# Reordering the attention stage of a hybrid residual block: the two heads of a pair one after the other on ScalarE, half a gate item between their suffix sums

## The reference

```
xn = rmsnorm(x); proj = xn @ w_in          # q,k,v of A | q,k,v, i, f, o of B | q of C | 3 x 1024 gate columns
A  stick-breaking attention, 8 heads x 64, causal (s < t):
   z = q k / 8;  log_keep = log_sigmoid(-z);  suffix = sum of log_keep over later s
   a = exp(log_sigmoid(z) + suffix);  y_sb = a v
B  mLSTM, 4 heads x 128, then rmsnorm per head and sigmoid(o):  y_ml
C  attention on 256 memory tokens, 4 heads x 128, q and k normed, softmax:  y_mem
merged = sum over branches of sigmoid(gate_b) * (y_b @ w_b);  h = x + merged @ w_out
h = h + PEER(rmsnorm(h))                   # 16384 one-neuron experts, 8 heads, top 16
```

## Time and profile before

| | us |
|---|---|
| median of three runs | 1521.15 (1515.63 to 1523.68) |
| the profiled execution | 1526.73 |
| its span | 1525.0 |
| PE busy | 1482.0 (97%) |
| DVE busy | 1103.5 (72%) |
| ACT busy | 749.7 (49%) |
| POOL busy | 423.0 (28%) |

### The profile page before, as it was taken

The page is one execution under the profiler, slowest core; times in us unless marked ns, Lnnn a source line. Parts: engine busy times, 40 slices in busy tenths (PEclk is TensorE's granted clock), DMA queues, the critical chain, the costliest instruction groups (busy, mean ns, idle before and its releaser), DMA issues.

```text
span 1525.0 us, 22189 instructions
## 1 busy us (share of the span) xinstructions
PE 1482.0 (97%) x7430; PEld 1216.5 (80%) x7430; DVE 1103.5 (72%) x1890; ACT 749.7 (49%) x939; POOL 423.0 (28%) x188
## 2 busy tenths in 40 slices
PE   7989999999889999999999999999999999999999
PEld 5768777777768888888888888888888888888887
DVE  6884542774957999999699999544666666666665
ACT  6343476646544544444465655544444444444442
POOL 4656523433545578779300000000000000000000
PEclk9999999999989999999999999999999999999999
DMA  5434533325633366666588888897988888888984
GB/s 195 159 122 143 198 104 104 104 83 217 239 124 111 111 214 221 207 215 219 204 311 300 290 315 304 310 322 241 326 293 285 296 285 288 294 285 290 299 280 147
DMA packets 166704, 345.14 MB, mean 226 GB/s; under 512 B 13420, under 2 KB 78956, under 8 KB 164336
## 3 DMA queue, kind: packets, MB, share of 16 engines
q1 hardware_dynamic: 166640, 344.32, 66.3%
HBM read 268.76 MB, written 75.51 MB: 226 GB/s over the span
## 4 chain that ended last, share of the span: by engine, by line
PE 65%; DVE 13%; issue 1%; POOL 1%; ACT 1%; ACTq 0%
PE ps L1144 30%; PE ps L1135 24%; PE ps L1173 4%; PE ps L728 2%; PE ps L1016 1%; DVE top_lists L1967 1%; DVE top_lists L1960 1%; POOL u_r L495 1%; DVE top_in L1961 1%; DVE top_lists L1964 1%; DVE top_lists L1957 1%; DVE mergedT L1890 1%; PE ps L751 1%; DVE h_scaled L1920 1%; PE ps L690 1%
## 5 line engine op out<-in xcount | busy, mean ns | idle before, releaser
L1135 PE MATMUL ps<-hT_r,u_r 128*128 128x512 f32 x2048 | 470.7, 390 | 0.1
L1144 PE MATMUL ps<-v_r,w_pairs 128*128 128x512 f32 x2036 | 461.7, 389 | 0.0
L1135 PEld LDWEIGHTS ps<-hT_r,u_r 128*128 128x128 f32 x2048 | 382.7, 188 | 79.8 <-POOL u_r L495 0.5
L1144 PEld LDWEIGHTS ps<-v_r,w_pairs 128*128 128x128 f32 x2036 | 382.3, 188 | 79.2
L459 POOL TENSOR_TENSOR w_r<-w_raw,w_r 128x1024 fp32r<-128x1024 f32 x93 | 238.5, 2569 | 263.6 <-ACT w_r L1259 174.4
L2106 DVE TENSOR_TENSOR v_r<-vraw,v_r 128x1024 fp32r<-128x1024 f32 x128 | 156.9, 1226 | 148.3 <-ACT v_r L1549 148.3
L1549 ACT ACTIVATE v_r<-vraw 128x1024 fp32r<-128x1024 f32 x128 | 135.7, 1060 | 253.6 <-PE ps L1144 248.7
L1496 ACT ACTIVATE act_stage<-ps 128x512 f32<-128x512 f32 x128 | 76.6, 599 | 227.6 <-PE ps L1135 227.6
L495 POOL TENSOR_TENSOR u_r<-uraw,u_r 128x1024 fp32r<-128x1024 f32 x60 | 172.9, 2892 | 46.7 <-ACT u_r L1477 46.4
L728 PE MATMUL ps<-xT_r,w_r 128*128 128x512 f32 x648 | 158.8, 400 | 8.6 <-DVE pre_stage L1703 4.4
L1259 ACT ACTIVATE w_r<-w_raw 128x1024 fp32r<-128x1024 f32 x99 | 103.9, 1055 | 104.2 <-PE ps L751 46.7
(11 more groups left out here) (261 smaller groups left out, 1510.4 us busy)
## 6 DMA issues: line engine op xcount, KB each, us to landing
uraw<-in_u SPq DMA_DIRECT2D x128, 512.0 KB, 4.7
vraw<-in_v SPq DMA_DIRECT2D x128, 512.0 KB, 5.3
w_raw<-in_w SPq DMA_DIRECT2D x100, 512.0 KB, 3.5
acts_out<-act_stage SPq DMA_DIRECT2D x128, 256.0 KB, 2.3
gates<-stage SPq DMA_DIRECT2D x16, 2048.0 KB, 7.4
g_in<-gates SPq DMA_DIRECT2D x64, 512.0 KB, 6.4
act_in<-acts_out SPq DMA_DIRECT2D x128, 256.0 KB, 5.3
gates_pre<-pre_stage SPq DMA_DIRECT2D x24, 256.0 KB, 2.4
```

The costliest lines, as they stand in the source:

```text
L1135: ins = pe.matmul(bank(s % 2), u2[s][:, w, k * P:(k + 1) * P], hr4[:, w, k, :], start=i == 0, stop=i == 15, skip_group_check=True)
L1144: ins = pe.matmul(bank(2 * q + h), w2[:, s, w, q * P:(q + 1) * P], v2[s][:, w, h * BANK:(h + 1) * BANK], start=start and w == 0, stop=stop ...
```

## The change

On PE `gate_item` is split in `gate_high` and `gate_low`; in each pair the high half of gate item m+2 goes between the suffix sums of the two heads. On ACT the heads of a pair go one after the other: Abs, Exp and Ln of the first, a weight item, Abs and Exp of the second, the high copy of the first, Ln of the second, a weight item, the high copy of the second; the two Exp of the sums and the third weight item as before. On DVE `take_y(p-1)` and the low part of the first head go ahead of the second `keep`, and `take_gate(m+1)` ahead of the second `low_part`. The norms of mem_q and mem_k go to the ends of the first and second pair. Behind the pairs `take_gate(16)` goes ahead of `decay(3)` and `take_gate(20)` ahead of the reduction; the gating of y_ml goes ahead of `take_gate(23)`; the low part of y_sb goes behind the third head's take in branch C. ACT makes the high part of the third branch item ahead of the high part of y_mem, which now waits for the first low part of `y_r`.

```diff
--- before.py
+++ after.py
@@ -822,11 +822,22 @@
                     n_item(n, n % 2, j, 4 * (1 - b % 2), xr4, TT)
             pe.wait_ge(n_out, 3 * TT)
 
-            def gate_item(m):
+            def gate_high(m):
 
                 at_least(pe, pre_out, m - (m == GATE_ASIDE))
                 n = gate_at(m)
-                t_item(n, n % 2, gate_bank(m), xr4)
+                high_ready(n)
+                t_part(n % 2, gate_bank(m), xr4, 0)
+
+            def gate_low(m):
+
+                n = gate_at(m)
+                take_item(n)
+                t_part(n % 2, gate_bank(m), xr4, 1)
+
+            def gate_item(m):
+                gate_high(m)
+                gate_low(m)
 
             for j in range(4):
                 n_item(V_AT[j], V_AT[j] % 2, j, 4, mr4, MT)
@@ -904,8 +915,9 @@
                 sb_suffix(2 * p)
                 if p == PAIRS - 1:
                     turn_rows()
+                gate_high(m + 2)
                 sb_suffix(2 * p + 1)
-                gate_item(m + 2)
+                gate_low(m + 2)
             pe.wait_ge(cols_out, 1)
             sb_values(PAIRS - 1)
             gate_item(16)
@@ -939,7 +951,7 @@
                 gate_item(18 + h)
 
 
-            pe.wait_ge(qk_normed, 1)
+            pe.wait_ge(qk_normed, 2)
             pe.wait_ge(num_out, MLH)
             for h in range(NH):
                 for t in range(TT):
@@ -1319,17 +1331,17 @@
             def region(s):
                 return ps[:, s * 3 * BANK:s * 3 * BANK + CAUSAL]
 
-            def ln_pair(p):
-
-                act.wait_ge(z_ready, p + 1)
-                for h in range(2):
-                    step(act.activation(lk[h], region(h), ACT.Abs))
-                for h in range(2):
-                    act.wait_ge(act_step, steps[0] - 1)
-                    step(act.activation(lk[h], lk[h], ACT.Exp, scale=-1.0))
-                for h in range(2):
-                    act.wait_ge(act_step, steps[0] - 1 + h)
-                    act.activation(lk[h], lk[h], ACT.Ln, bias=1.0).then_inc(ln_ready, 1)
+            def abs_part(h):
+
+                step(act.activation(lk[h % 2], region(h % 2), ACT.Abs))
+
+            def exp_abs(h):
+                act.wait_ge(act_step, steps[0])
+                step(act.activation(lk[h % 2], lk[h % 2], ACT.Exp, scale=-1.0))
+
+            def ln_part(h):
+                act.wait_ge(act_step, steps[0])
+                act.activation(lk[h % 2], lk[h % 2], ACT.Ln, bias=1.0).then_inc(ln_ready, 1)
 
             def hi_part(h):
                 act.wait_ge(*((keep_ready, h + 1) if h < 2 else (keep_summed, h - 1)))
@@ -1346,11 +1358,18 @@
 
             act.activation(roots[:, 61:62], eps_col[:, :], ACT.Exp)
             for p in range(PAIRS):
-                ln_pair(p)
                 n = I_G + GATES_IN_KV + 3 * p + 2
+                act.wait_ge(z_ready, p + 1)
+                abs_part(2 * p)
+                exp_abs(2 * p)
+                ln_part(2 * p)
+                high_ws(n)
+                abs_part(2 * p + 1)
+                exp_abs(2 * p + 1)
                 hi_part(2 * p)
+                ln_part(2 * p + 1)
+                high_ws(n + 1)
                 hi_part(2 * p + 1)
-                high_ws(n, n + 1)
                 exp_part(2 * p)
                 exp_part(2 * p + 1)
                 high_ws(n + 2)
@@ -1368,7 +1387,7 @@
             act.activation(roots[:, S_ML:S_H], sums[:, S_ML:S_H], ACT.Sqrt, bias=eps_col[:, :],
                            scale=1.0 / HD).then_inc(ml_rooted, 1)
             high_ws(I_G + 22)
-            act.wait_ge(qk_normed, 1)
+            act.wait_ge(qk_normed, 2)
             for h in range(NH):
                 act.wait_ge(qkT_done, h + 1)
                 act.activation(mem_qT3[:, h, :], bank(h), ACT.Copy, scale=qg_scaled[:, 0:1]).then_inc(qkT_out, 1)
@@ -1409,8 +1428,9 @@
 
             act.wait_ge(mlT_out, MLH)
             act.activation(y_r[:, 4096:6144], y_mlT, ACT.Copy, scale=1.0 / SPREAD).then_inc(y_hi, 1)
+            high_w(I_BR + 2, (I_BR + 2) % 4)
             act.wait_ge(my_out, NH)
-            act.wait_ge(y_lo, 2)
+            act.wait_ge(y_lo, 1)
             act.activation(y_r[:, 8192:10240], y_memT, ACT.Copy, scale=1.0 / SPREAD).then_inc(y_hi, 1)
 
 
@@ -1429,9 +1449,10 @@
                                scale=1.0 / SPREAD).then_inc(m_hi, 1)
 
             for p in range(12):
-                high_w(I_BR + p + 2, (I_BR + p + 2) % 4)
                 if p == 0:
                     gate_of(0)
+                else:
+                    high_w(I_BR + p + 2, (I_BR + p + 2) % 4)
                 if p >= 9:
                     merged_hi(p - 9)
                 if p < 11:
@@ -1715,18 +1736,21 @@
             for t in range(MT):
                 dve.tensor_scalar(mem_v3[:, t, :], bank(4 + t), rstd[:, TT + t:TT + t + 1], None,
                                   ALU.mult).then_inc(n_out, 1)
-            dve.wait_ge(qk_rooted, 1)
-            link(dve.reciprocal(rstd[:, S_Q:S_ML], roots[:, S_Q:S_ML]))
+            take_gate(3)
 
             def spread(col, n, m):
 
                 return col.unsqueeze(2).broadcast_to([P, n, m])
 
-            q_ = mem_q.rearrange("p (g c) -> p g c", c=HD)
-            k_ = mem_k.rearrange("p (g c) -> p g c", c=HD)
-            dve.tensor_tensor(q_, q_, spread(rstd[:, S_Q:S_K], 16, HD), ALU.mult)
-            dve.tensor_tensor(k_, k_, spread(rstd[:, S_K:S_ML], 8, HD), ALU.mult).then_inc(qk_normed, 1)
-            take_gate(3)
+            def norm_q():
+                dve.wait_ge(qk_rooted, 1)
+                link(dve.reciprocal(rstd[:, S_Q:S_ML], roots[:, S_Q:S_ML]))
+                q_ = mem_q.rearrange("p (g c) -> p g c", c=HD)
+                dve.tensor_tensor(q_, q_, spread(rstd[:, S_Q:S_K], 16, HD), ALU.mult).then_inc(qk_normed, 1)
+
+            def norm_k():
+                k_ = mem_k.rearrange("p (g c) -> p g c", c=HD)
+                dve.tensor_tensor(k_, k_, spread(rstd[:, S_K:S_ML], 8, HD), ALU.mult).then_inc(qk_normed, 1)
 
             def region(s):
                 return ps[:, s * 3 * BANK:s * 3 * BANK + CAUSAL]
@@ -1771,22 +1795,26 @@
                 m = GATES_IN_KV + 3 * p
                 take_gate(m)
                 keep(2 * p)
-                keep(2 * p + 1)
-                low_part(2 * p)
                 if p >= 1:
                     take_y(p - 1)
+                low_part(2 * p)
+                keep(2 * p + 1)
+                take_gate(m + 1)
                 low_part(2 * p + 1)
-                take_gate(m + 1)
                 if p == PAIRS - 1:
                     dve.wait_ge(cols_turned, 1)
                     dve.tensor_copy(key_cols[:, :], bank(6)[:, 0:32]).then_inc(cols_out, 1)
                     decay(0)
                     decay(1)
                 take_gate(m + 2)
+                if p == 0:
+                    norm_q()
+                elif p == 1:
+                    norm_k()
             take_y(PAIRS - 1)
             decay(2)
+            take_gate(16)
             decay(3)
-            take_gate(16)
 
             def weigh(h):
                 dve.wait_ge(e_masked, h + 1)
@@ -1819,17 +1847,22 @@
                     take_gate(18)
             dve.wait_ge(num_out, MLH)
             link(dve.tensor_tensor(squares, y_ml, y_ml, ALU.mult))
+            take_gate(20)
             dve.tensor_reduce(sums[:, S_ML:S_H], squares.rearrange("p (g c) -> p g c", c=HD), AX.X,
                               ALU.add).then_inc(ml_squared, 1)
-            take_gate(20)
-            dve.wait_ge(ml_rooted, 1)
-            link(dve.reciprocal(rstd[:, S_ML:S_H], roots[:, S_ML:S_H]))
             y_ = y_ml.rearrange("p (g c) -> p g c", c=HD)
-            link(dve.tensor_tensor(y_, y_, spread(rstd[:, S_ML:S_H], 16, HD), ALU.mult))
-            dve.wait_ge(sig_o, 1)
-            dve.scalar_tensor_tensor(out=y_ml, in0=y_ml, scalar=SPREAD, in1=ml_o, op0=ALU.mult,
-                                     op1=ALU.mult).then_inc(ml_normed, 1)
-
+
+            def scale_ml():
+                dve.wait_ge(ml_rooted, 1)
+                link(dve.reciprocal(rstd[:, S_ML:S_H], roots[:, S_ML:S_H]))
+                link(dve.tensor_tensor(y_, y_, spread(rstd[:, S_ML:S_H], 16, HD), ALU.mult))
+
+            def gate_ml():
+                dve.wait_ge(sig_o, 1)
+                dve.scalar_tensor_tensor(out=y_ml, in0=y_ml, scalar=SPREAD, in1=ml_o, op0=ALU.mult,
+                                         op1=ALU.mult).then_inc(ml_normed, 1)
+
+            scale_ml()
             take_gate(21)
 
 
@@ -1848,11 +1881,14 @@
                 p_ = probs[h % 2].rearrange("p (t m) -> p t m", m=MEM)
                 dve.tensor_tensor(p_, p_, spread(den[:, 16 + n4:20 + n4], 4, MEM), ALU.mult).then_inc(mp_ready, 1)
 
+            def low_y(b):
+                dve.wait_ge(y_hi, b + 1)
+                dve.scalar_tensor_tensor(out=y_r[:, b * 4096 + 2048:(b + 1) * 4096],
+                                         in0=y_r[:, b * 4096:b * 4096 + 2048].bitcast(F32), scalar=1.0 - SPREAD,
```

(20 more changed lines are left out.)

## The result

| | before | after |
|---|---|---|
| median, us | 1521.61 (four runs, 1515.63 to 1523.68) | 1532.32 (four runs, 1531.67 to 1533.82) |
| the profiled execution, us | 1526.73 | 1533.82 |
| its span, us | 1525.0 | 1532.1 |
| ScalarE, GpSimd busy, us | 749.7, 423.0 | 760.5, 418.1 |

The account below looks back on a forecast made before the run. TensorE was taken as what everything waits for in the attention stage; work terms summed to +4.5 us, slow clock added 6: +10.5, rounded to +10 on the median 1521.15, so 1531 us, 8 in 10 range 1517 to 1539.

Parts of the forecast that it names:

- Entry: First pair: moving the norms lets TensorE go on 2.5 us earlier, all given back; next pair's gate item +1.7 us.
- The take behind the second keep: In each pair, VectorE's late emptying of bank 7 makes TensorE wait before the gate half; the take is 4.6 us late.
- The cycle at full clock: One pair after the change, without slow clock: 27.8 us with 6.2 us of pauses, against 23.4 us in the old order.
- Table loads: ScalarE in each pair: every change between Exp and Ln costs a load, four instead of two, 16 in the stage.
- The clock: One slow-clock stretch of 1.5 us behind each of four long TensorE pauses: +6 us, bounds 0 and +12.
- The last pair: Fourth pair, to the first mLSTM scores: 31.1 us instead of 28.62, +2.5 us before any slow clock.
- mLSTM, memory, to the third branch item: Behind the pairs, earlier takes, moved gating and low part, and an earlier weight copy: -0.6, -0.4 and -3.4 us.
- From 458 us on: The change touches nothing from 458 us to the end; a change there of more than 2 us would show it wrong.
- rival of spared pairs: Pairs: POOL does not hold the small sums, each of three pairs 1.9 us shorter, clock possibly spared; about 1523 us, chance 0.30.
- rival of table sets: ScalarE in the pairs: one set serves Exp and Ln, so all loads inside the pair go; 1517 us, chance 0.10.
- That of the slow clock: Pairs: TensorE stays at the lower clock through most of the suffix sums, +6 us more; 1537 us, chance 0.10.

Follow-up runs that it names:

- the pauses filled: The changed kernel with sixteen never-read matmuls behind the first head's suffix sums in pairs 2 to 4: 1527.26 us, ratio 1.0039 to the kernel before.

## Why the prediction was right, point by point

The forecast was the case that came: 1531 us with +10.5, measured 1532.32 with +10.7. Against its own profiled execution the sum was too high, though, +10.5 against +7.1 of span, so part of the agreement is luck: the profiled execution of before lay 5.1 us above its median, that of after 1.5 us above its own, which returns the 3.6 us. By the traces, 2.3 us of the excess lie in the pairs: 8.9 and 6 us of slow clock were forecast for them, 14.9 in all, and 12.6 measured. Another 0.9 us is that the stage began earlier in the execution of after (it begins between 183.4 and 185.6 us in the kept traces). What follows the pairs came as forecast, -4.4 us by the out-projection.

- **Entry.** The 2.5 us won are all given back, as forecast: ratio 1.0004 for the norms alone, though there in part to the clock and not to ScalarE. From the first pair's scores to the second pair's gate item the change costs 2.12 us (26.66 to 28.78); forecast 1.7 and a slow stretch of 1.5. The forecast had 3.8 us of pause for the high copy (measured 3.69) and 1.8 for the take, which did not come: the sums ahead of it ran at the slow clock for so long.
- **The take behind the second keep.** The step that decided. TensorE paused 4.37 us for a forecast of 4.6. The additions were held 1.7 us and ended with GpSimd's part, 17.5 us behind the first Abs (forecast 18.1 for them held, 18.8 for the take; the take ended at 18.1). Moving the take or the copy each removes a part, both together three quarters.
- **The cycle at full clock.** Forecast 27.8, measured 27.23 with the pauses filled. For the old order the prediction had 23.4, and a pair without a slow stretch takes 23.22. The first head's sums did not win: the high copy ended 10.95 us behind Abs (forecast 11.2). A pair of additions of the first head, at 220.08, was held as well (2.47 us), which the working did not see; it had slack. So had the norm of q, which took 4.00 us where at most 3.4 was said.
- **Table loads.** 16 for a forecast of 16, each 1.28 us. By the Trainium skill (ScalarE: Activation LUTs, Table sets: the hidden batching unit) Exp and Ln in turn share one load, since one set has both; the trace of after disagrees once more, with a load at every change between them. (The load at 227.11 that the prediction cites does not stand right behind Ln: two high copies and two weight copies come between.) The kernel with two loads per pair was 7.9 us faster, though not by the loads alone, since GpSimd's hold on the second additions went with them.
- **The clock.** Forecast 1.5 us per pair, 6 in all. Against the kernel with the pauses filled, pairs 2 to 4 lost 1.4, 2.3 and 1.3 us, so 1.7 us per pair; the first pair was not filled. Stretches of 3.4 and 6.8 us fall differently from one execution to the next: the old pairs have 13.7 us of slow clock in the trace of before and 6.8 in that of the part behind alone. No row tells which pause brings which.
- **The last pair.** +2.5 and a slow stretch of 1.5 forecast, +3.20 measured (28.62 to 31.82).
- **mLSTM, memory, to the third branch item.** Forecast -0.6, -0.4 and -3.4. From 303.12 to the first transpose at 350.98 it is -1.24 in two steps (-1.03 and -0.21); to the low half of the third item, 40 matmuls behind 370.02, it is -3.5.
- **What was not forecast.** The pause of 2.78 us at the fifth branch item, where ScalarE's copy waits for DMA. By the out-projection the stage had given back 0.3 us of the 3.5, since other pauses ahead of it went. Alone, the part behind the pairs gave 3.2 us, not 4.4.
- **From 458 us on.** The signs said a change under 2 us; 24 matmuls of the expert stage start 7.08 us late (458.91 to 465.99) and the span ends 7.1 us late.

The rival of spared pairs (1523) fell with the 4.37 us pause, the rival of table sets with the 16 loads. That of the slow clock (1537) overshot by 5 us.

## What to carry to other kernels

Half a filler item belongs where its buffer has already been emptied. Between the two heads, where it waited for a take, it stands in a kernel that loses 0.98% against the same kernel with the old pairs; ahead of both heads it stands in one that gains 0.56% (0.9927 against 0.9983). Not all of that is its place, since ScalarE's order differs too. The nearest pair of kernels has the same order on ScalarE and differs only in the place of the half item and in VectorE's order: 1.0029 with it between the heads, 0.9927 with it ahead. Before two chains are staggered on one engine, count what each change of function costs there and look at which queue the second chain's helpers stand in; here the stagger brought two loads more per pair and set a GpSimd operation beside the two additions that TensorE's pause hung on. Pauses of TensorE are to be priced at more than their length, by the slow stretches that follow them: here 1.3 to 2.3 us for a pause of about 4. And where the DMA engines are full, as behind the pairs here, part of a freed pause can come back as a wait for data.

## What the runs showed of the hardware

- Two additions of 128 columns on SBUF take 0.75 us, and 2.41 us beside one GpSimd subtraction of 2.34 us. The Trainium skill (SBUF — State Buffer, SBUF: two separate sides) has it that VectorE with two SBUF inputs and GpSimd shut each other out for a whole instruction; the trace agrees, the second pair ends 0.61 us behind GpSimd's part (230.28, 230.89). `keep`, which reads one operand from PSUM, took its usual 1.48 us beside a GpSimd part of 2.38 us (219.33 and 218.33 us in the kernel with the half item ahead).
- Sixteen matmuls that nobody reads in a pause of about 4 us, in three such places, made the kernel 5.1 us faster between the medians (6.4 by the ratios): the clock stayed at 2.4 GHz there.
- At 412 GB/s the DMA engines are full (share 1.01 and 1.03), and the reader of a 512 KB load then waited 5.29 us for it.
